# The output stage of a decoder block: routing table in float32r parts, rows turned before they are normalized, another TensorE order, four weight slabs loaded early

## What is computed

```python
h = h + merged @ w_out[layer]
xf = rms_norm(h, ffn_norm_w[layer]).reshape(N, D)
logits = xf @ router_w + router_b
top_logit, top_idx = lax.top_k(logits, TOP_K)          # 4 of 32
gate = jax.nn.softmax(top_logit, axis=-1)
# each expert: its tokens, in order of token, with their gates
gu = x_blk @ w_gate_up[e] + b_gate_up[e]
act = (u + 1.0) * (g * jax.nn.sigmoid(SWIGLU_ALPHA * g))
y = act @ w_down[e] + b_down[e]
out = h.at[token].add(y * gate)
```

## Time and profile before

| what | us |
|---|---|
| median of 3 runs | 2264.84 |
| lowest, highest | 2262.13, 2267.14 |
| the profiled execution: its time | 2266.68 |
| the profiled execution: span of the trace | 2264.9 |
| TensorE busy in it | 2159.7 (95%) |
| output stage in it, first matmul to last DVE instruction | 730.2 to 876.1 |
| first product of the expert stage | 892.07 |

### The profile page before, as it was taken

The page is one execution under the profiler, slowest core; times in us unless marked ns, Lnnn a source line. Parts: engine busy times, 40 slices in busy tenths (PEclk is TensorE's granted clock), DMA queues, the critical chain, the costliest instruction groups (busy, mean ns, idle before and its releaser), DMA issues.

```text
span 2264.9 us, 38947 instructions
## 1 busy us (share of the span) xinstructions
PE 2159.7 (95%) x13792; PEld 1674.4 (74%) x13793; DVE 1612.5 (71%) x1572; ACT 1323.2 (58%) x1484; POOL 589.3 (26%) x513
## 2 busy tenths in 40 slices
PE   7899999999888996999999999999999999999997
PEld 7877777677667784777777777787887777777775
DVE  4065757576466344888887887797998778777787
ACT  4166666757444112666766766676776666566665
POOL 1311101111156002124543522232432222112222
PEclk9999999999989997999999999999999999999998
DMA  4101202121266324998999998898999989888894
GB/s 149 29 29 46 75 26 68 33 69 49 66 206 203 124 95 168 374 353 290 342 346 315 348 344 312 300 398 299 396 376 321 304 303 323 304 297 299 308 328 119
DMA packets 268389, 517.24 MB, mean 228 GB/s; under 512 B 33909, under 2 KB 78400, under 8 KB 268316
## 3 DMA queue, kind: packets, MB, share of 16 engines
q1 hardware_dynamic: 242012, 472.95, 57.9%
q0 software_dynamic: 17088, 39.14, 6.9%
q10 hardware_dynamic: 9216, 4.20, 0.7%
HBM read 476.87 MB, written 43.50 MB: 230 GB/s over the span
## 4 chain that ended last, share of the span: by engine, by line
PE 56%; DMA 1%; SPq 1%; issue 1%; DVE 0%; ACT 0%; POOL 0%; ACTq 0%; POOLq 0%; DVEq 0%
PE ex_gu L2133 29%; PE ex_yp L2177 15%; PE ex_rest L2155 6%; PE ex_rest L2194 3%; PE ex_gu L2085 1%; SPq L1696 1%; PE ex_tr L2093 1%; PE ex_gu L2093 1%; DMA ex_bias<-bp_s 1%; PE ex_gu L2120 0%; DMA ex_raw<-in_w_gate_up_dram 0%; DVE ex_wlo L2003 0%; PE ex_tr L2085 0%; PE ex_yp L2124 0%; ACT ex_whi L1743 0%
## 5 line engine op out<-in xcount | busy, mean ns | idle before, releaser
L2003 DVE TENSOR_TENSOR ex_wlo<-ex_raw,ex_whi 128x2048 fp32r<-128x2048 f32 x387 | 873.7, 2289 | 198.0 <-ACT ex_whi L1743 197.1
L1743 ACT ACTIVATE ex_whi<-ex_raw 128x2048 fp32r<-128x2048 f32 x387 | 733.9, 1927 | 183.8 <-PE ex_gu L2133 123.3
L2133 PE MATMUL ex_gu<-ex_whi,ex_xhi 128*128 128x512 f32 x1024 | 284.3, 399 | 1.0 <-DVE ex_xlo L2044 1.0
L2133 PE MATMUL ex_gu<-ex_whi,ex_xlo 128*128 128x512 f32 x1024 | 274.6, 390 | 0.0
L2133 PE MATMUL ex_gu<-ex_wlo,ex_xhi 128*128 128x512 f32 x1024 | 274.1, 390 | 0.0
L2133 PEld LDWEIGHTS ex_gu<-ex_whi,ex_xhi 128*128 128x128 f32 x1024 | 186.4, 188 | 56.9 <-issue 20.6
L2133 PEld LDWEIGHTS ex_gu<-ex_whi,ex_xlo 128*128 128x128 f32 x1024 | 192.7, 188 | 41.0
L2133 PEld LDWEIGHTS ex_gu<-ex_wlo,ex_xhi 128*128 128x128 f32 x1024 | 192.2, 188 | 40.5
L705 POOL TENSOR_TENSOR at_wlo<-at_raw,at_whi 128x1024 fp32r<-128x1024 f32 x29 | 71.7, 2473 | 426.7 <-ACT at_whi L520 426.7
L57 PE MATMUL at_job<-xnT_hi,at_whi 128*128 128x512 f32 x416 | 179.6, 432 | 2.1 <-ACT at_rs L555 2.1
L59 PE MATMUL at_job<-xnT_hi,at_wlo 128*128 128x512 f32 x416 | 164.8, 396 | 0.0
(11 more groups left out here) (312 smaller groups left out, 3630.4 us busy)
## 6 DMA issues: line engine op xcount, KB each, us to landing
ex_raw<-in_w_gate_up_dram SPq DMA_DIRECT2D x512, 512.0 KB, 8.4
ex_raw<-in_w_down_dram SPq DMA_DIRECT2D x256, 512.0 KB, 8.0
at_raw<-in_w_in_dram SPq DMA_DIRECT2D x25, 512.0 KB
gT<-at_gst SPq DMA_DIRECT2D x32, 256.0 KB, 2.3
mg_g<-gT SPq DMA_DIRECT2D x32, 256.0 KB, 4.0
n_x<-in_x_dram SPq DMA_DIRECT2D x8, 512.0 KB, 11.0
y_s<-at_yst ACTq DMA_DIRECT2D x64, 64.0 KB, 1.6
ring<-y_s SPq DMA_DIRECT2D x8, 512.0 KB, 6.0
```

What stands on the lines that cost most here:

```text
L1743: nc.scalar.activation(w_hi[:, i % RING, :], raw[:, i % SLABS, :], ACT.Copy).then_inc(hi_d, 1)
L2003: nc.vector.tensor_tensor(w_lo[:, slot, :], raw[:, i % SLABS, :], w_hi[:, slot, :].bitcast(F32), ALU.subtract).then_inc(lo_d, 1)
L2133: mm = nc.tensor.matmul(gu[:, half, h, :], x[:, k, :], w[:, kk, h, :], start=half == 0 and k == 0 and n == 0, stop=k == KD - 1 and n == 2)
```

## The change

- The slot table's product is made of float32r parts in a single pass. `rt_slot` and `rt_held` are float32r; `rt_held` has four groups of 32 columns in place of two (high and low part of the token number, high and low part of the gate), the table 128 rows in place of 64. The parts of the gate are made by two more small DVE instructions, and two more fill `rt_held`. The two parts are added where the table is turned, by a product with `rt_pair_sum`, which holds ones.
- Rows are turned before they are normalized. PE turns `op_h`; the norm's weights are multiplied into the router's weights once (POOL, with `op_wcol`, which eight transfers of one column of 128 numbers each bring); the reciprocal root comes in where the logits are read (one DVE instruction with bias). `op_xn` is still made and stored, by DVE for tiles 0 to 6 and by two POOL instructions for tile 7.
- PE's order: both halves of tile 0; then for each t: a quarter of t+1's projection (12 matmuls), turn t, two quarters, logits t, table of t-1, the last quarter, ranks of t. DVE's order for each t: `residual(t)`, `hand_out(t-1)`, `normalize(t)`, logits and `choose(t)`.
- Slabs 0 to 3 of the first expert are loaded in the output stage: 0 and 1 after tile 0's stores, 2 and 3 after the store of the last `op_xn`. `raw_o` and `ring` are moved to the place where `ex_raw` begins, since they are the first to be done with. The expert stage's SP loads biases, waits for the gathered rows, and loads slabs 4 to 11.

```diff
+                for k in range(KD):
+                    sp.dma_start(wcol[:, k:k + 1], ffn_norm_w[0:1, k * P:(k + 1) * P].rearrange("a (p b) -> (a p) b", b=1))\
+                        .then_inc(c_in, 16)
...
                 for t in range(NT):
+                    if t == 1:
+                        sp.wait_ge(wlo_d, KD - EARLY)
+                        for i in range(2):
+                            load_gate_up(sp, w_gate_up, slab_raw, slab_in, i, 0)
                     sp.wait_ge(h_done, t + 1)
...
+                sp.wait_ge(mm_done, NT)
+                for i in range(2, 4):
+                    load_gate_up(sp, w_gate_up, slab_raw, slab_in, i, 0)
...
                 for t in range(NT):
+                    if t:
+                        gates(t - 1)
+                        act.wait_ge(sq_done, t)
                     act.wait_ge(h_done, t + 1)
...
+                pool.wait_ge(c_in, 48 + 16 * KD)
+                nc.gpsimd.tensor_tensor(rw[:, :, :], rw[:, :, :], wcol[:, :].rearrange("p (k o) -> p k o", o=1)
+                                        .to_broadcast([P, KD, NE]), ALU.mult).then_inc(c_set, 1)
...
+                nc.gpsimd.tensor_scalar(xn[:, (NT - 1) % 2, :], ht[:, (NT - 1) % 2, :], rstd[:, NT - 1:NT], None, ALU.mult)\
+                    .then_inc(rstd_done, 1)
...
+                nc.gpsimd.tensor_tensor(xn[:, (NT - 1) % 2, :], xn[:, (NT - 1) % 2, :], wB[:, :], ALU.mult)\
+                    .then_inc(xn_done, 1)
...
-                    nc.vector.tensor_tensor(held[:, s, :, 1, :], oh[:, s, :, :], each(mine, NE), ALU.mult).then_inc(sl_d, 1)
+                    step(nc.vector.tensor_copy(gate_hi[:, :], mine))
+                    step(nc.vector.tensor_tensor(gate_lo[:, :], mine, gate_hi[:, :].bitcast(F32), ALU.subtract))
+                    step(nc.vector.tensor_tensor(held[:, s, :, 2, :], oh[:, s, :, :], each(gate_hi[:, :].bitcast(F32), NE),
+                                                 ALU.mult))
+                    nc.vector.tensor_tensor(held[:, s, :, 3, :], oh[:, s, :, :], each(gate_lo[:, :], NE), ALU.mult)\
+                        .then_inc(sl_d, 1)
...
+                dve.wait_ge(c_set, 24 + Q)
                 for t in range(NT):
+                    residual(t)
                     if t:
                         hand_out(t - 1)
+                    if t < NT - 1:
+                        normalize(t)
...
+                for t in range(NT):
+                    project(t + 1, 0, 0)
+                    turn(t)
+                    project(t + 1, 0, 1)
+                    project(t + 1, 1, 0)
+                    route(t)
                     if t:
                         take_slots(t - 1)
+                    project(t + 1, 1, 1)
                     rank_tokens(t)
                 take_slots(NT - 1)
```

More of the change, by code:

```diff
@@ L1541, in take_slots @@
                     for j in range(TOPK):
-                        last = nc.tensor.matmul(table[0:2 * NE, 0:2 * P],
+                        last = nc.tensor.matmul(table[:, 0:2 * P],
                                                 held[:, t % 2, j, :, :].rearrange("p c e -> p (c e)"),
@@ L2228, in _ @@
             for h in range(2):
-                last = nc.tensor.transpose(tr[:, 2 * NE * h:2 * NE * (h + 1)], rt["table"][:, h * P:(h + 1) * P],
-                                           ident[0:2 * NE, 0:2 * NE])
+                last = nc.tensor.matmul(tr[:, 2 * NE * h:2 * NE * (h + 1)], rt["table"][:, h * P:(h + 1) * P],
+                                        rt["pair_sum"][:, :], start=True, stop=True)
             last.then_inc(t_tr, 1)
```

132 lines of the change are left out of this document (73 added, 59 removed).

## The result

The changed kernel takes 2252.97 us at the median of six runs (2249.87 to 2257.75), the kernel before beside it 2265.69 (2262.13 to 2267.32, six runs). The ratio is 0.9949, with a 95% interval of 0.9936 to 0.9962: 8.6 to 14.5 us less. The forecast was 9.3 less. The profiled execution took 2254.18, with a span of 2252.1.

What follows compares the result with a forecast made beforehand. TensorE's own work bounds the loop and expert stage, a chain through all engines the stretch behind the last projection. -2.9 - 9.1 + 3.8 - 1.1 = -9.3, median 2255.5 us, range 2249.5 to 2260.5.

Steps and rivals of the forecast that it cites:

- The loop: Output stage's tile loop, up to the last residual: one more turning, logits, ranking and table, all tables cheaper; -2.9 us.
- POOL's hold: Tail: POOL's two normalization instructions for the last tile make DVE stand, so the logits are read later; +3.8 us.
- the first expert's -1.1: Expert stage: with slab 3 already present, TensorE goes on sooner ahead of the bias products; -1.1 us.
- the single-pass product: Slot table's product, in the loop: four float32r matmuls take 0.6 us in place of 1.9 for a table.
- What the order puts in: Loop: one more turning (0.8), set of logits (2.0), ranking (0.2) and table (0.6) ahead of the last residual.
- The tail alone: Chain behind the last projection, from last residual to the table's copy, without POOL's hold; -9.1 us.
- waits to 856.1, and reaches the next as POOL has begun its second: to 858.6: Tail: DVE held at `rt_gate_lo` by POOL's first instruction, then by its second; logits read at 859.2, not 855.4.
- C: Rival: every product at its dearer end, with clock 0.68 from before the last logits; +3.6, 2259.1 us; 14%.
- A: Rival, tail: POOL's instructions hold nothing, so the +3.8 is gone; 2251.7 us; 17%.
- B: Rival, tail: POOL's first instruction takes 1.2 in place of 3.0, so +2.0; 2253.7 us; 12%.
- D: Rival: the table's single pass is none, six tables at 1.9 and the last at 3.8; 2265.7 us; 4%.
- E: Rival, start of output stage: late column loads hold up DVE's first residual; 2269.9 us if landing at 765; 3%.

Runs made afterwards that it cites:

- r6: Changed kernel with the tile loop's order of TensorE, DVE and ACT put back to that of before; 2259.98 us in one run.
- r5: Changed kernel with the operands of the slot table's product in plain float32, still as four groups; 2265.28 us in one run.
- r12: Changed kernel with last tile normalized by DVE behind its choice of experts, 35 idle matmuls in the tail, first slab split behind `ex_xlo`; 2251.25 us, six runs.
- r2: The changed kernel once more, nothing edited; 2255.33 us.
- r3: Changed kernel with the last tile normalized by one DVE instruction in place of two on POOL; 2249.49 us at the median of four runs.
- r7: Changed kernel with three more POOL instructions of no use behind its last normalization, 128x1024, two SBUF inputs each; 2261.3 us in one run.
- r8: Changed kernel with three more POOL instructions of no use behind its last normalization, 128x1024, one SBUF input each; 2259.88 us in one run.
- r9: Changed kernel with 35 matmuls of no use in TensorE's gaps behind the last residual, to keep its clock up; 2249.12 us in one run.
- r4: Changed kernel with slabs 0 to 3 loaded in the expert stage again, as before the change; 2252.04 us in one run.
- r1: The kernel before once more, nothing edited; 2265.4 us.
- r10: Changed kernel with DVE normalizing the last tile, 35 idle matmuls in the tail, 44 before the gathered rows' turning, first slab split delayed; 2258.12 us, nine runs.
- r11: As r10, but with no slab loaded early and no delay of the first split; 2256.56 us, six runs.

## Why the prediction came out as it did

**The sum was near, and its errors partly cancel.** Predicted -9.3; what repeats in the marks is -4.2 in the loop and -6.7 in the tail, -10.9, and nothing clear of scatter for the first expert. The measured -12.7 has an interval that covers this. The loop's gain was forecast 1.3 too small and that of the tail with POOL's hold (-9.1 and +3.8) 1.4 too small; the first expert's -1.1, which is not there, took part of that back. That much of the near hit was luck.

**The loop: -2.9 predicted, -4.2 measured.** The mis-sized term is the single-pass product. I gave it 1.3 less than the float32 one (0.6 for 1.9), five times between the residuals. r6, which has this product and the order of before, is 7.85 below before for those five, 1.57 each: 1.3 in the product's own slot, 0.1 in the logits, and the rest at the joints of instructions around it, where I had assumed no gain. r5 gives less, 1.27 each, because float32 with 128 weight columns took 1.62 from start to start and not the 1.87 of before. What the order puts in was right: 3.6 predicted, 3.67 between r6 and the changed kernel. Its largest part was read too high, though: the 842.87 of the earlier trace rows is the first weight load of the logits, and from product to product a set costs 1.79 before and 1.70 now, not 2.0; what made up for it is projections cut in four instead of two.

**The tail alone: 14.05 from last residual to copy predicted, 13.75 in r12.** In r12 the last table at clock 1.00 takes 0.5 off, and DVE's normalization in the chain adds about 0.4 by its rows, so the two can be compared. The chain was right, down to the table inputs (4.27 measured, 4.25 predicted) and the last table (1.33, 1.4 predicted). The logits at 2.3 were wrong in the profiled execution (3.60 at clock 0.50) and near in r2 (1.94).

**POOL's hold: +3.8 predicted, about +1.7 to +2.5 measured.** By r3 it is 1.7, against 14.05 it is 2.5. It depends on the logits: in the changed kernel they end at 853.73 and one DVE instruction behind them is held for 1.0, in r2 DVE comes earlier and stands for 2.2. POOL's end was forecast at 9.0 behind the last residual and came at 9.12. The step that failed is "waits to 856.1, and reaches the next as POOL has begun its second: to 858.6". The one-input instruction lets DVE through in its middle, so the table's inputs were done before the second began; and under the second, DVE still read the logits from PSUM, took the maximum and searched the index, which I had put behind POOL's end. They make 1.1 to 1.4 that come off. The reading of the earlier trace rows that it rests on adds up by a 0.56 that stands in no row (alone the instruction takes 0.69); that DVE goes on at POOL's end is shown by r7 instead. Also wrong was that equal fillings of 0.29 speak against tensor-scalar being held: both had been measured with POOL idle, and a duration without the rival says nothing of a port.

**C was right in its cause and wrong in its price.** The clock did fall ahead of the logits, in the changed kernel and in r8. It cost nothing there, since POOL's end came later still: r2, r7 and r9, with logits of 1.94, have `rt_oh` at 9.18 to 9.22, r4 and r5, with 2.11 and 2.34, at 9.18 and 9.17, the changed kernel and r8, with 3.60 and 3.59, at 9.25. Two late things on parallel branches don't add.

**A fell by the stretched instructions, B by POOL's first taking 2.85, D by the table's 0.56, E by landing times:** the first residual came 17.6 to 20.9 into the stage, before 19.2 and 19.7, and in the changed kernel the eight column loads had landed by 739.7, 7.9 ahead of it (POOL's product of weights starts then).

**The first expert: -1.1 predicted, about 0 measured.** Slab 3's wait in the earlier trace rows belonged to that execution and not to the kernel; r1 and r4, with slabs loaded late, don't have it. "The path to the gathered rows is unchanged" was wrong twice: POOL's copy waits 0.87 for DVE, and the gather, with no slabs under way beside it, is 0.4 to 0.9 shorter than in r4 and the two traces before. I had asked what the early slabs delay on SP and the DMA queues, and not what DVE now does earlier with them, nor what their absence gives the gather.

## What to carry to other kernels

Work given to POOL on the critical tail is paid twice if it is wide and reads two SBUF operands: by its length, and by every DVE cast, tensor-scalar or two-input instruction that meets it. Place it where DVE reads PSUM, reduces or waits. When two branches meet, cost the later one only, and before a wait of one trace goes into a sum, look for it in a second execution. Data that arrives early wakes its consumers early: ask what they share with the path, and what the transfers moved away had been slowing.

## What the runs showed of the hardware that I had not expected

- A POOL instruction with one input stopped DVE for its first 1.12 to 1.25 us, let it through, and stopped it again near its end (r8, changed kernel); one with two inputs stopped it for all of its 2.35.
- A gather took 5.4 us from issue to turning with a DMA share of 0.26 beside it, and 5.8 to 6.3 with one of 0.95 and more (changed kernel; r4 and before).
- The hold works both ways: POOL's 128x4 copy took 1.06 for 0.19 under a DVE split; POOL's third idle instruction in r7 took 3.20 for 2.35 behind DVE's `rt_slot`.
- TensorE's granted clock at the same place of the tail was 1.00 in one execution and 0.50 in another of one kernel (logits 1.94 and 3.60).
- 88 further matmul records in a wait of 11 us were followed by a pause of 6.6 us ahead of the next product (r10, r11).
